# Hybrid RG-LRU and mLSTM trunk on one core: a norm multiplied through by its denominator, weight buffers mapped to other state chunks, and the first head's gate rows in another order

## The reference, cut to what matters

```
num = inter * (q @ C) + S @ v          # S: masked scores times exp(Dm - m_t)
den = inter * (q @ n) + sum(S)
h   = num / max(|den|, exp(-m_t))
C_new = scale * C + kw^T @ v ;  n_new = scale * n + sum(kw)
h   = h * rsqrt(mean(h*h, over the head's 512 columns) + EPS)     # EPS = 1e-6
h   = h * norm_g ;  y = (sigmoid(o_pre) * h) @ w_out
```

## Time and profile before

| | us |
|---|---|
| median of 3 runs (2006.12 to 2010.9) | 2008.05 |
| the profiled execution, its own time | 2011.13 |
| its span, first to last instruction | 2009.4 |
| PE busy | 1910.8 |
| DVE busy | 729.6 |
| ACT busy | 720.0 |
| POOL busy | 817.6 |

### The profile page before, as it was taken

How to read it: one execution, slowest core, us unless ns; L and a number is a source line. 1 busy time by engine, 2 the same in 40 slices (tenths; PEclk the granted TensorE clock), 3 DMA queues, 4 the chain that set the end, 5 groups by cost and what they waited for, 6 DMA issues and landing times.

```text
span 2009.4 us, 35922 instructions
## 1 busy us (share of the span) xinstructions
PE 1910.8 (95%) x13703; PEld 1768.6 (88%) x13703; DVE 729.6 (36%) x862; ACT 720.0 (36%) x1049; POOL 817.6 (41%) x683
## 2 busy tenths in 40 slices
PE   6999899999999998999999989899999999999997
PEld 6999799999999998998544645899999999999996
DVE  5677522111111122477677577221221111111213
ACT  3476733332222224443432332332443322222332
POOL 4242354553553544564110100453655535544442
PEclk7999999999999999999899999899999999999998
DMA  3232223222222222422378677321332222222212
GB/s 112 74 90 74 63 82 90 83 84 82 81 84 83 79 83 63 88 70 98 114 245 280 215 243 261 127 90 59 89 90 84 84 83 80 84 84 81 82 60 72
DMA packets 187003, 209.44 MB, mean 104 GB/s; under 512 B 24459, under 2 KB 150035, under 8 KB 186847
## 3 DMA queue, kind: packets, MB, share of 16 engines
q1 hardware_dynamic: 186250, 207.41, 33.6%
q10 hardware_dynamic: 648, 0.59, 0.1%
HBM read 167.31 MB, written 40.64 MB: 103 GB/s over the span
## 4 chain that ended last, share of the span: by engine, by line
PE 76%; DVE 7%; issue 6%; POOL 4%; ACT 4%; DMA 2%; ACTq 0%; POOLq 0%; SPq 0%; DVEq 0%
PE ps L2128 65%; POOL W_LO L636 3%; PE ps L2350 2%; PE ps L2411 2%; DVE C_HALVES L1934 2%; PE ps L2389 1%; POOL SQUARE_SUM L644 1%; DMA out_ml_C_s_dram<-C_HALVES 1%; DVE H_PAD L1642 1%; PE ps L2284 1%; DMA C_HALVES<-in_state_mlstm_C_dram 1%; PE ps L2466 1%; DVE SQUARE_SUM L1971 1%; PE ps L2344 0%; ACT W_HI L947 0%
## 5 line engine op out<-in xcount | busy, mean ns | idle before, releaser
L636 POOL TENSOR_TENSOR W_LO<-W_RAW,W_HI 128x512 fp32r<-128x512 f32 x464 | 609.1, 1323 | 691.8 <-ACT W_HI L947 691.5
L947 ACT ACTIVATE W_HI<-W_RAW 128x512 fp32r<-128x512 f32 x484 | 297.7, 628 | 732.1 <-PE ps L2128 723.2
L2128 PE MATMUL ps<-A_HI,W_HI 128*128 128x288 f32 x2304 | 498.1, 298 | 18.5 <-POOL W_LO L636 10.0
L2128 PE MATMUL ps<-A_LO,W_HI 128*128 128x288 f32 x2304 | 495.7, 297 | 0.0
L2128 PE MATMUL ps<-A_HI,W_LO 128*128 128x288 f32 x2304 | 495.2, 297 | 0.0
L2128 PEld LDWEIGHTS ps<-A_HI,W_HI 128*128 128x128 f32 x2304 | 373.7, 190 | 21.5 <-issue 17.4
L2128 PEld LDWEIGHTS ps<-A_LO,W_HI 128*128 128x128 f32 x2304 | 373.7, 190 | 0.0
L2128 PEld LDWEIGHTS ps<-A_HI,W_LO 128*128 128x128 f32 x2304 | 373.2, 190 | 0.0
L1693 DVE TENSOR_TENSOR X<-X,ps 128x1152 f32 (+1 forms) x36 | 48.7, 1354 | 341.2 <-PE ps L2128 341.2
L2128 PE MATMUL ps<-G_HI,W_HI 128*128 128x288 f32 x704 | 151.0, 296 | 2.5 <-POOL G_LO L745 2.5
L2128 PE MATMUL ps<-G_LO,W_HI 128*128 128x288 f32 x704 | 150.7, 296 | 0.0
(11 more groups left out here) (377 smaller groups left out, 2441.8 us busy)
## 6 DMA issues: line engine op xcount, KB each, us to landing
W_RAW<-in_ffn_w_up_dram SPq DMA_DIRECT2D x176, 256.0 KB, 2.8
C_HALVES<-in_state_mlstm_C_dram SPq DMA_DIRECT2D x64, 512.0 KB, 4.9
out_ml_C_s_dram<-C_HALVES SPq DMA_DIRECT2D x64, 512.0 KB, 5.2
W_RAW<-in_ffn_w_down_dram SPq DMA_DIRECT2D x88, 256.0 KB, 2.6
W_RAW<-in_ml_w_in_dram SPq DMA_DIRECT2D x64, 256.0 KB, 2.7
W_RAW<-in_rg_w_in_dram SPq DMA_DIRECT2D x48, 256.0 KB, 2.8
W_RAW<-in_ple_w_gate_dram SPq DMA_DIRECT2D x32, 256.0 KB, 2.6
W_RAW<-in_ml_w_out_dram SPq DMA_DIRECT2D x32, 256.0 KB, 2.8
```

The source lines that it names most:

```text
L636: pool.tensor_tensor(W_LO[:, s], W_RAW[:, s], W_HI[:, s].bitcast(F32), ALU.subtract).then_inc(lo_ready, 1)
L947: act.activation(W_HI[:, s], W_RAW[:, s], ACT.Copy).then_inc(hi_ready, 1)
L2128: ins = pe.matmul(ps[:, 4 * s + 2 * m + h, 0:HALF_T], a[:, w, k, wc], x[:, h * HALF_T:h * HALF_T + HALF_T], start=i == 0 and k == 0 and q ...
```

## The change

It has three parts.

The norm: `inverses` goes away. ACT squares d, scaled by the square root of EPS, into `SCALE_F` as soon as `denominators` is done (`square_denominators`); `square_mean` becomes one instruction that adds the sum of squares over 512 to it; `root_mean` is a bare root; `normalise` loses the product with 1/d.

The slots: `W_RAW` moves behind `W_HI` and `W_LO` in memory, so slots 0 and 1 lie under `W_HI`, 2 and 3 under `W_LO`, 4 and 5 under `W_RAW`.

The first head: q's banks are copied out by ACT and DVE, two each, and all four of k by DVE; k's large projection comes before its small one; the input gate row is formed after the k copies; ACT's `key_stack(0)` moves behind the exponentials, and DVE's `k_stack_lo(0)` behind the decay exponents; `sel0` moves to bank 1 and `sel2` to bank 0; `sel1` and its copy are dropped, and `EXP_NEG_M` comes by a DMA that SP issues right behind the three stores of the rows. The last DMA counts on `rows_spread`, hence the 16 more in the later heads' wait.

The diff, with one line of context:

```diff
--- before.py
+++ after.py
@@ -36,7 +36,7 @@
 HALVES = 2 * UNITS * HEADS
-RAW_SLOTS, HI_SLOTS, LO_SLOTS = (0, 1), (2, 3), (4, 5)
+HI_SLOTS, LO_SLOTS, RAW_SLOTS = (0, 1), (2, 3), (4, 5)
 STATES_STORED = [16 * (1 + len(range(slot, HALVES, CSLOTS))) for slot in range(CSLOTS)]
@@ -77,8 +77,8 @@
         return [("v0", (4,)), ("v1", (5,)), ("v2", (6,)), ("v3", (7,)), ("v4", (0,)), ("qt", UNIT_BANKS), ("gates", (2, 3)),
-                ("qs", (1,)), ("gate_rows", (2, 3)), ("ks", (0,)), ("kt", UNIT_BANKS), ("sc0", (2,)), ("st", (4, 5)), ("sc13", (3,)),
-                ("vs", (6, 7)), ("cols", (0,)), ("sel0", (4,)), ("sel2", (5,)), ("sc2s", (1,)), ("sel1", (0,)), ("u0", UNIT_BANKS),
+                ("qs", (1,)), ("gate_rows", (2, 3)), ("kt", UNIT_BANKS), ("ks", (0,)), ("sc0", (2,)), ("st", (4, 5)), ("sc13", (3,)),
+                ("vs", (6, 7)), ("cols", (0,)), ("sel0", (1,)), ("sel2", (0,)), ("sc2s", (1,)), ("u0", UNIT_BANKS),
                 ("r0", (2,)), ("r1", (3,)), ("r2", (1,)), ("r3", (2,)), ("pv0", (3,)), ("u1", UNIT_BANKS), ("pv1", (1,))] \
@@ -212,9 +212,9 @@
         with ExitStack() as pw:
-            W_RAW = sb_in(pw, "W_RAW", [P, 4, 2, 256])
             W_HI = sb_in(pw, "W_HI", [P, 4, 2, 256], F32R)
             W_LO = sb_in(pw, "W_LO", [P, 4, 2, 256], F32R)
+            W_RAW = sb_in(pw, "W_RAW", [P, 4, 2, 256])
         with ExitStack() as pc:
@@ -362,6 +362,7 @@
         v_stack_hi, kw_hi, k_sums = sem("v_stack_hi"), sem("kw_hi"), sem("k_sums")
+        den_squared = sem("den_squared")
         v_neg, rows_stored, rows_spread = sem("v_neg"), sem("rows_stored"), sem("rows_spread")
@@ -563,6 +564,7 @@
             sp.wait_ge(rows_stored, 48)
+            sp.dma_start(EXP_NEG_M[:, 0:SEQ], ROWS_KEPT[0:1, T:T + SEQ].broadcast_to([P, SEQ])).then_inc(rows_spread, 16)
             for h in range(HEADS):
@@ -1318,7 +1320,14 @@
                 act.wait_ge(bank_freed[bank], FREED[h, name, bank])
-                act.activation(SCALE_F[:, t0:t0 + n], SCALE_F[:, t0:t0 + n], ACT.Sqrt, bias=EPS_COL[:, :], scale=1.0 / HD).then_inc(sd_ready, 1)
+                act.activation(SCALE_F[:, t0:t0 + n], SCALE_F[:, t0:t0 + n], ACT.Sqrt).then_inc(sd_ready, 1)
+
+            def square_denominators(h):
+
+                for name in ("den", "ds"):
+                    bank = at(h, name)
+                    act.wait_ge(bank_freed[bank], FREED[h, name, bank])
+                act.activation(SCALE_F, DEN, ACT.Square, scale=EPS ** 0.5).then_inc(den_squared, 1)
 
@@ -1341,6 +1350,8 @@
 
+            query(0, 0)
+            query(0, 1)
             act.wait_ge(piece_done, DONE[0, "gates"])
@@ -1349,10 +1360,8 @@
             act.activation(ABS_F[:, :], ABS_F[:, :], ACT.Ln, bias=1.0).then_inc(ln_ready, 1)
-            act.wait_ge(piece_done, DONE[0, "kt"])
-            bank = BANKS[0, "kt"][3]
-            act.activation(K_T[:, 3, 0:SEQ], ps[:, bank, :], ACT.Copy).then_inc(bank_freed[bank], 1)
             sample_columns(0, "ks", K_T)
+            sample_columns(0, "qs", Q_T)
             bank = at(0, "ks")
@@ -1362,7 +1371,6 @@
             ins.then_inc(k_stack_in, 1)
-            key_stack(0)
             act.wait_ge(t1_ready, 1)
@@ -1373,6 +1381,7 @@
             ins.then_inc(rows_ready, 1)
+            key_stack(0)
 
@@ -1382,9 +1391,6 @@
                     exps_(0)
-                    bank = at(0, "sel1")
-                    act.wait_ge(piece_done, DONE[0, "sel1"])
-                    act.activation(EXP_NEG_M[:, 0:SEQ], ps[:, bank, :], ACT.Copy).then_inc(bank_freed[bank], 1)
                 else:
@@ -1412,6 +1418,7 @@
                     gains(3)
+                square_denominators(h)
                 prompt_state(h, 0)
@@ -1808,7 +1815,7 @@
             dve.tensor_scalar(RUN_NEG[:, :], RUN_MASK[:, :], 1.0, -NEG, ALU.subtract, ALU.mult)
-            for c in range(4):
+            for c in range(2, 4):
                 bank = BANKS[0, "qt"][c]
@@ -1817,14 +1824,11 @@
             dve.tensor_scalar(F_ROW[:, :], F_ROW[:, :], GATE_BIAS[:, 1:2], None, ALU.add).then_inc(f_ready, 1)
+            for c in range(4):
+                key(0, c)
             dve.tensor_scalar(I_ROW[:, :].rearrange("p (h n) -> p h n", h=2), pg[0:4], GATE_BIAS[:, 0:1], None, ALU.add).then_inc(bank_freed[2], 1)
...
             dve.nop().then_inc(bank_freed[3], 1)
-            for c in range(3):
-                key(0, c)
-            bank = at(0, "qs")
-            dve.wait_ge(piece_done, DONE[0, "qs"])
-            dve.tensor_copy(Q_T[:, :, SEQ:T], ps[:, bank, 0:4 * N_STOK].rearrange("p (c t) -> p c t", c=4)).then_inc(bank_freed[bank], 1)
             dve.wait_ge(ln_ready, 1)
@@ -1845,20 +1849,20 @@
             dve.tensor_scalar(HEAD_SEL[:, :], ONES[0:HEADS, :], IDENT[0:HEADS, 0:1], None, ALU.mult).then_inc(sel_ready, 1)
-            k_stack_lo(0)
 
...
                 dve.wait_ge(piece_done, DONE[h, name])
-                dve.tensor_tensor(SCALE_F[:, t0:t0 + n], SCALE_F[:, t0:t0 + n], ps[:, bank, c0:c0 + n], ALU.mult).then_inc(bank_freed[bank], 1)
+                dve.wait_ge(den_squared, h + 1)
+                scale = SCALE_F[:, t0:t0 + n]
+                dve.scalar_tensor_tensor(scale, ps[:, bank, c0:c0 + n], 1.0 / HD, scale, ALU.mult, ALU.add).then_inc(bank_freed[bank], 1)
 
...
                 link(dve.reciprocal(scale, scale))
-                link(dve.tensor_tensor(scale, scale, DEN[:, t0:t0 + n], ALU.mult))
                 for c in range(4 * h, 4 * h + 4):
@@ -1876,7 +1880,7 @@
                 else:
-                    dve.wait_ge(rows_spread, 80 * h)
+                    dve.wait_ge(rows_spread, 16 + 80 * h)
                     for i in (1, 2, 3):
@@ -1953,6 +1957,8 @@
                 bank = at(h, "den")
+                if h == 0:
+                    dve.wait_ge(rows_spread, 16)
                 dve.wait_ge(piece_done, DONE[h, "den"])
@@ -1966,12 +1972,6 @@
 
-            def inverses():
-
-                link(dve.reciprocal(DEN, DEN))
-                dve.tensor_tensor(SCALE_F, DEN, DEN, ALU.mult).then_inc(dve_step, 1)
-                step.adv()
-
             bank = at(0, "cols")
@@ -1983,6 +1983,7 @@
                     decay_exponents(0)
+                    k_stack_lo(0)
                     v_stack_lo(0)
@@ -2012,9 +2013,7 @@
                 update(h, 4)
-                inverses()
                 update(h, 5)
-                dve.wait_ge(dve_step, step.now())
                 square_mean(h, "hp", 0, 0, SEQ)
@@ -2503,8 +2502,8 @@
             done(0, "gate_rows", ins)
+            projection(0, "k")
             sample_projection(0, "k")
-            projection(0, "k")
             first_scores(0)
@@ -2520,7 +2519,6 @@
             scores_2s(0)
-            broadcast("sel1", EXP_ROW)
             for h in range(HEADS):
```

## The result

The changed kernel takes 2033.42 us (median of 4 runs, 2031.12 to 2038.13) against 2009.47 for the kernel before in the same session (2006.12 to 2010.96). The ratio is 1.0114, 95% interval [1.0086, 1.0142]: slower by about 24 us, where 9 us of gain were forecast. Its profiled execution took 2038.13 us with a span of 2036.4 us, 27.0 more than before.

A forecast was written before the change was run, and what follows sets the result against it. PE was taken to bound the kernel (76% of the chain). Gains of 4.0 (heads), 0.9 (first stretch), 3.7 (tail) and 0.8 (clock) summed to 9.4 us: 2001.7 from the profiled 2011.13, 1998.7 from the median; range 1993.5 to 2004.0.

The forecast's parts named there:

- The heads: Four heads of the mLSTM stage: the shorter norm gains 1.6, 0.4, 0 and 2.0 us, together 4.0.
- The long wait is gone everywhere: PE's wait for DVE at u6, 1.66 us in head 0 and 1.95 in head 3, disappears in all heads.
- What is late next is u7: At u7 in each head: its second load, behind half 10's store and the five broadcasts, limits the gain to 0 to 2.0 us.
- my first rival: All heads: state loads pace every head, so the 4.0 us fall away; gain 5.4 us, 2002.7 us, chance 0.13.
- The slower rival: Heads: PE's stop moves from u6 to u7, before its thinnest work, and the clock falls; 2012.7 us, chance 0.04.
- The first stretch: Before head 0's updates: sc0 earlier 0.5, sel1 gone 1.8, sc2s waiting for DVE 1.4 lost; gain 0.9 us.
- The tail: Behind the last head: exchanged slots let W_HI start earlier, gain 3.7 us, PE's gap shrinking from 6.7 to about 3.0.
- The clock behind it: After the gap behind the last head: a shorter fall to half clock gains 0.8 us, from 0 to 2.5.
- The added square: ACT, once d is ready in each head: squaring 576 values takes 0.8 us, covered by ACT's idle time.

The follow-up runs named there:

- e10: Changed kernel with three of cp3's four products moved directly behind u7, then cn, the fourth product and nt; 2014.03 us, ratio 1.0009 to the kernel before.
- e13: Kernel before with the changed norm, broadcasts two halves later and cp3 split two and two around u7, old slots and first head kept; 1999.88 us, ratio 0.9928.
- e15: Repeat of e11, the same kernel measured again beside e13 and e14; 1990.61 us, ratio 0.9897 to the kernel before.
- e11: Changed kernel with the five broadcasts two halves later and two of cp3's four products ahead of u7, two between nt's; 1992.83 us, ratio 0.9920 to before.
- e12: e11 with the norm of the kernel before (reciprocal, square and product back on DVE); 2004.97 us, ratio 0.9969 to the kernel before.
- e5: Changed kernel with all four of cp3's products moved ahead of u7, leaving nt alone behind it; 2006.92 us, ratio 0.9968 to the kernel before.
- e14: e11 with one of cp3's products ahead of u7 and three behind, instead of two and two; 1991.14 us, ratio 0.9888 to the kernel before.
- e2: Changed kernel with the old norm put back, so only the slots and first head differ from the kernel before; 2007.90 us, ratio 0.9986.
- e6: Changed kernel with SP's five broadcasts for the next head issued two halves later; 2007.75 us, ratio 0.9969 to the kernel before.
- e8: Changed kernel with one extra 512-column product, whose result is overwritten, added on PE between cp2 and u7; 2027.90 us, ratio 1.0054 to the kernel before.
- e7: Changed kernel storing only the first of the two sequences of each half, leaving out half of the state's store; 2005.55 us, ratio 0.9962 to before.
- e3: Changed kernel with three extra 512-column products, whose results are overwritten, added on PE between cp2 and u7; 2004.45 us, ratio 0.9969 to the kernel before.

## Why the prediction was wrong

**The heads: the term failed, in size and in sign.** Predicted was a gain of 4.0 us, measured is a loss of 35.0. The sum has no term for what a new stop ahead of u7 does to the clock; the runs show 23.9 us at half clock behind it in each of heads 0 to 2. Three steps stand apart.

- "The long wait is gone everywhere": right. Waits for DVE fell by 7.0 us, the two-per-head pattern became one short wait at u5.
- "What is late next is u7": right in place, wrong in what it gives. I let the load gain 1 to 2 us in head 0 (1.6 taken), 0.4 in head 1 and 2.0 in head 3. From update u4's store to u7 it is the same to 0.3 us in all four heads, so the mechanism of my first rival, that the loads pace every head, was the true one (I gave it 0.13); its 2002.7 us was nearly as far off, for it had no clock in it either. The store and the load behind it stood in the earlier trace rows for head 2, and I took them for that head's own. In head 1 the chain of the earlier trace rows went through update u5, but only just: the store had landed at 1094.54, 0.65 us ahead of the load's issue at 1095.19, and what those 0.65 us gave the load lost again on its way.
- The step that failed is the one I did not take: the stop that had to appear. I wrote that PE would be ready 3.3 us earlier in head 0 and the load 1 to 2 us earlier, so a stop of about 2 us more ahead of u7 was on paper. I priced its time, nothing, and not its clock. The slower rival had this mechanism (PE's stop moves from u6 to u7, ahead of its thinnest work, and the clock falls), and I set its chance at 0.04 because "head 1 has small stops too and kept its clock". Head 1's stop at u7 was 0.58 us; the new ones are 1.7 to 3.7. A small stop that cost nothing is no evidence for a large one.

**The size within that rival.** I put 7 us at half clock a head without a row for it; the falls in my rows stand ahead of dense work, cp2 in head 0 and 4.97 us of slabs. Behind u7 it is 23.9 us, and e10 halves that by order alone. At half price 23.9 us are 12.0 a head; measured are 9.8 in head 1, for a small product does not take twice as long at half clock (0.69 us against 0.43, 1.06 against 0.63).

**The first stretch.** Predicted 0.9, measured 2.05. sc0 started 0.66 us earlier, near the 0.5 of the sum, and ran at full clock, which the bound of 1.7 us had allowed. That it did is luck as far as the runs tell: sc0 is at half clock in some of the kernels and not in others, and here the fall came 12 us later. sc2s waits 1.27 us for DVE, predicted 1.4.

**The tail.** Predicted 3.7 and 3.0 of gap left: the gap shrank by 3.68 to 3.00. The clock behind it was 0.66 over the first 4.97 us where it was 0.50; with the whole rest 2.27 us came back, where 0.8 was the value and 2.5 the bound. The gap stands in e13 against e15 too (6.29 and 2.98 us). The clock does not, it is 0.50 over the first 4.97 us in both: in the changed kernel it had fallen 17 us before the gap's end, behind head 3's u7, and so came back sooner. That part of the gain is luck.

**The added square** takes 0.68 us on ACT, predicted 0.8, and no wait for it shows.

The sum of the parts outside the heads was 5.4 by forecast and 8.0 by the windows of the two profiled executions. The error of 39 us in the heads is one mechanism.

## What to carry to other kernels

- When a wait is removed, say where PE will stand instead and what it does right behind that place. Here a stop of 1.9 us ahead of dense products cost 1.5 to 1.7 us or nothing beyond itself; stops ahead of a stretch of thin products cost 9 to 12 us a head, each time from 2.7 us on and about every other time below. Price a stop by what follows it.
- Work that can be ordered freely (here a quarter of the prompt's state) belongs in front of the wait that stays; half of it there, and the broadcasts two halves later, turned a loss of 1.1% into a gain of 1%.
- If a stream of transfers paces a stage, measure from the transfer that starts its chain to the instruction that needs it. If that distance does not depend on the engine you relieve, relieving it only moves the stop. The distance is not a constant, though: with the broadcasts out of the way the shorter norm did bring u7's load forward (landed 9.5 to 10.9 us behind that store's issue in e11, 10.8 to 12.4 in e12).

## What the runs showed of the hardware that I had not expected

- One stop of 2.69 us was followed by 23.9 us at half clock although PE then had no idle time (14.01 and 7.45 us busy in windows as long, clock 0.50). With three of cp3's products right behind u7 instead (e10, head 2) the first fall lasted 3.4 us.
- Thin work can lose the clock with no stop at all, for 10 to 14 us in e5 and e11, for 17.1 in head 1 of e14.
- Of middling stops ahead of u7 some kept the clock (1.86 us before, 1.84 in e2, 2.01 in e6) and some lost it (1.77 in e8, 1.01 in e7, 0.75 in e14). Runs of one kernel differ by it: e6 from 1994.6 to 2014.8 us, with the mean granted clock going along. The kernel before does it too: 21 of its 31 runs beside e6 took 2005 to 2013 us at a mean clock of 0.976 to 0.981, nine took 2015 to 2025 us at 0.968 to 0.974. What decides was not settled.
- The DMA engines moved 378 GB/s over 7.7 us of e3 and 382 over 3.9 us of e10, loads and stores together. Between the kernel before and the changed one the distance from update u4's store to u7 kept to 0.3 us in each head although DVE had 4.4 us less to do; a load issued earlier into this stream took longer.
